# A fused two-block network on one core: the first weight unit loaded and split in halves, the order of VectorE's and ScalarE's work at the start of the expert stage, and one gate multiplication at the end

## The reference, cut to what matters

```python
def swiglu(h, w_in, w_out):
    gate, up = jnp.split(h @ w_in, 2, axis=-1)
    return (jax.nn.silu(gate) * up) @ w_out

def first_block(x, ...):                      # depth 2
    h = h + 0.5 * swiglu(rmsnorm(h, norm_ffn1[i]), ffn1_w_in[i], ffn1_w_out[i])
    ...                                       # conv or dilated attention, then another swiglu

def second_block(x, c, ...):
    mod = jax.nn.silu(c) @ mod_w[l] + mod_b[l]
    ...                                       # h = h + gate_m * hybrid_mixer(...)
    xf = _rms_norm(h, norm_ffn_w[l]) * (1.0 + scale_f) + shift_f
    h = h + gate_f * _hierarchical_moe(xf, ...)
    return _rms_norm(h, norm_out_w)

def _hierarchical_moe(xm, ...):
    # softmax over 4 groups, top 1; softmax over its 4 experts, top 2; comb = their weights
    for gi in range(N_GROUPS_2):
        act = jax.nn.silu(hg) * hu * comb[:, gi, :, None]
        out = out + jnp.einsum('tef,efd->td', act, w_down[gi])
```

## Time and profile before

| | us |
|---|---|
| median of three runs | 1887.58 |
| the profiled execution's own time | 1887.4 |
| its span | 1885.2 |
| TensorE busy | 1849.6 (98%) |
| VectorE busy | 1220.2 (65%) |
| ScalarE busy | 943.4 (50%) |
| mean granted TensorE clock | 0.988 of full |

### The profile page before, as it was taken

How to read it: one execution, slowest core, us unless ns; L and a number is a source line. 1 busy time by engine, 2 the same in 40 slices (tenths; PEclk the granted TensorE clock), 3 DMA queues, 4 the chain that set the end, 5 groups by cost and what they waited for, 6 DMA issues and landing times.

```text
span 1885.2 us, 24482 instructions
## 1 busy us (share of the span) xinstructions
PE 1849.6 (98%) x9398; PEld 1529.7 (81%) x9398; DVE 1220.2 (65%) x1308; ACT 943.4 (50%) x1037; POOL 117.4 (6%) x142
## 2 busy tenths in 40 slices
PE   8999999999999999999999999999999999999997
PEld 6888998888888888888888888898988788876764
DVE  4566666566644557665556566787655766868677
ACT  5443435344544355544445434564445455667574
POOL 0100000000000000000100000223100050000000
PEclk9999899999999999999999999999999999999998
DMA  6877455777555547555644777544233357879695
GB/s 232 292 250 244 144 187 170 235 260 249 169 170 189 186 159 215 179 179 179 90 73 160 246 244 260 170 157 146 101 119 136 111 209 249 324 247 343 248 337 188
DMA packets 239272, 379.16 MB, mean 201 GB/s; under 512 B 13511, under 2 KB 149069, under 8 KB 239184
## 3 DMA queue, kind: packets, MB, share of 16 engines
q1 hardware_dynamic: 233728, 365.13, 57.0%
q0 software_dynamic: 5456, 12.81, 4.0%
HBM read 372.83 MB, written 10.30 MB: 203 GB/s over the span
## 4 chain that ended last, share of the span: by engine, by line
PE 93%; DVE 4%; ACT 1%; DMA 1%; issue 0%; SPq 0%; POOLq 0%; ACTq 0%; DVEq 0%
PE ps L374 27%; PE ps L376 27%; PE ps L375 27%; PE ps L1057 2%; PE ps L1079 1%; PE ps L2790 1%; PE ps L761 1%; PE ps L1067 1%; DVE lo L357 1%; PE ps L1548 1%; PE ps L1035 1%; ACT hi L351 0%; PE ps L1563 0%; PE ps L2837 0%; PE ps L488 0%; PE ps L811 0%
## 5 line engine op out<-in xcount | busy, mean ns | idle before, releaser
L357 DVE TENSOR_TENSOR lo<-raw,hi 128x2048 fp32r<-128x2048 f32 x296 | 679.1, 2299 | 323.2 <-ACT hi L351 322.2
L351 ACT ACTIVATE hi<-raw 128x2048 fp32r<-128x2048 f32 x296 | 565.3, 1915 | 370.0 <-PE ps L376 361.7
L374 PE MATMUL ps<-hi,xT_hi 128*128 128x512 f32 x1376 | 549.9, 400 | 8.1 <-DVE lo L357 5.6
L376 PE MATMUL ps<-hi,xT_lo 128*128 128x512 f32 x1376 | 538.2, 391 | 0.0
L375 PE MATMUL ps<-lo,xT_hi 128*128 128x512 f32 x1376 | 538.2, 391 | 0.0
L374 PEld LDWEIGHTS ps<-hi,xT_hi 128*128 128x128 f32 x1376 | 259.8, 189 | 62.1 <-DVE lo L357 6.1
L376 PEld LDWEIGHTS ps<-hi,xT_lo 128*128 128x128 f32 x1376 | 259.4, 188 | 56.0
L375 PEld LDWEIGHTS ps<-lo,xT_hi 128*128 128x128 f32 x1376 | 259.9, 189 | 49.4
L374 PE MATMUL ps<-hi,ffn_hhi 128*128 128x512 f32 x352 | 137.8, 391 | 0.0
L375 PE MATMUL ps<-lo,ffn_hhi 128*128 128x512 f32 x352 | 137.1, 389 | 0.0
L376 PE MATMUL ps<-hi,ffn_hlo 128*128 128x512 f32 x352 | 137.0, 389 | 0.0
(11 more groups left out here) (453 smaller groups left out, 2248.1 us busy)
## 6 DMA issues: line engine op xcount, KB each, us to landing
raw<-in_ffn_w_in SPq DMA_DIRECT2D x176, 512.0 KB, 4.5
raw<-in_ffn_w_out SPq DMA_DIRECT2D x88, 512.0 KB, 4.1
raw<-in_attn_w_qkv SPq DMA_DIRECT2D x72, 512.0 KB, 4.5
raw<-in_w_in SPq DMA_DIRECT2D x64, 512.0 KB, 4.3
modraw<-in_mod_w SPq DMA_DIRECT2D x48, 512.0 KB, 6.7
raw<-in_w_gate SPq DMA_DIRECT2D x48, 512.0 KB, 4.3
raw<-in_w_up SPq DMA_DIRECT2D x48, 512.0 KB, 5.4
raw<-in_w_down SPq DMA_DIRECT2D x48, 512.0 KB, 4.5
```

The lines of the kernel that those rows point to most:

```text
L351: nc.scalar.activation(hi[u % SPLIT][:, :], raw[raw_slot(u)][:, :], ACT.Copy).then_inc(S("hi_ready"), 1)
L357: nc.vector.tensor_tensor(lo[u % SPLIT][:, :], raw[raw_slot(u)][:, :], hi[u % SPLIT][:, :].bitcast(F32), ALU.subtract).then_inc(S("lo_read ...
L374: nc.tensor.matmul(dst, w_hi, x_hi, start=start, stop=False, skip_group_check=True)
L376: return nc.tensor.matmul(dst, w_lo, x_hi, start=False, stop=stop, skip_group_check=True)
```

## The change

Four things are altered.

1. *First unit in halves.* Unit 0 is loaded by four DMAs of 256 KB in place of two of 512 KB: k = 0, 1 of both column groups first (semaphore `first_half_loaded`), then k = 2, 3. ScalarE rounds it in two instructions of 128x1024 after parts 0 and 1 of `x` rather than one of 128x2048 after all four; VectorE splits it likewise, between parts 1 and 2. TensorE starts with k = 0, 1 of tile 0 once the first half is split, and waits for the whole unit before k = 2.
2. *Expert stage, position 1.* VectorE copies `gathered(1, 1)` and splits block 0's inner activations (`inner_lo(0)`) ahead of the rank tables, and copies `gathered(1, 3)` between the two token tiles' tables. ScalarE does `inner_hi(0)` ahead of rounding unit (1,3) rather than behind it.
3. *Expert stage, position 2.* The groups of `info` come one unit sooner on TensorE (after units (2,0), (2,1), (2,2) rather than (2,1), (2,2), (2,3)). VectorE does `inner_lo(3)`, then `block_info("info_rest", ...)`, then splits D0; before, it split D0, then did `block_info`, then `inner_lo(3)`.
4. *The end.* `y_back`'s copies are added for both tiles first; then the sums in PSUM are added to them, and one multiplication by the gate row and one addition to `h` per tile do for both. `add_gated` is no longer called here.

Some semaphores are also merged into others (`gd_ld` into `gd_small`, `cs_ready` and `conv_pad` into counters shared with the new ones); what waits for what is the same there.

```diff
         def round_unit(act, u, it=None, per=0):
-            if it is None and ("a", u) in done:
+            if it is None and (u == 0 or ("a", u) in done):
                 return
...
+        def first_unit_act(act):
+
+            act.wait_ge(S("first_half_loaded"), 32)
+            nc.scalar.activation(hi[0][:, 0:UNIT // 2], raw[0][:, 0:UNIT // 2], ACT.Copy).then_inc(S("first_half_hi"), 1)
+            act.wait_ge(S("raw_loaded0"), 32)
+            nc.scalar.activation(hi[0][:, UNIT // 2:UNIT], raw[0][:, UNIT // 2:UNIT], ACT.Copy).then_inc(S("hi_ready"), 1)
+
+        def first_unit_dve(dve):
+
+            dve.wait_ge(S("first_half_hi"), 1)
+            nc.vector.tensor_tensor(lo[0][:, 0:UNIT // 2], raw[0][:, 0:UNIT // 2], hi[0][:, 0:UNIT // 2].bitcast(F32),
+                                    ALU.subtract).then_inc(S("first_half_lo"), 1)
+            dve.wait_ge(S("hi_ready"), 1)
+            nc.vector.tensor_tensor(lo[0][:, UNIT // 2:UNIT], raw[0][:, UNIT // 2:UNIT], hi[0][:, UNIT // 2:UNIT].bitcast(F32),
                                     ALU.subtract).then_inc(S("lo_ready"), 1)
...
         def tok_unit(pe, u, half, banks, fresh=None, it=None, per=0, between=None):
 
-            pe_wait_unit(pe, u, it, per)
+            if u:
+                pe_wait_unit(pe, u, it, per)
+            else:
+                pe.wait_ge(S("first_half_lo"), 1)
...
+                if u == 0 and (t, k) == (0, 2):
+                    pe_wait_unit(pe, u, it, per)
...
+                if n == 0 and i == 1:
+                    first_unit_act(act)
...
+                if u == 0:
+                    for k in range(2):
+                        for g in range(2):
+                            sp.dma_start(dst[:, 2 * k:2 * k + 2, g, :], in_src(i, it, half, g)[:, 2 * k:2 * k + 2, :]).then_inc(
+                                S("raw_loaded0" if k else "first_half_loaded"), 16)
+                    return
...
-                    round_unit(act, u)
                     if n == 1 and i == 3:
                         inner_hi(0)
+                    round_unit(act, u)
...
                     split_unit(dve, u)
                     if n == 1 and i == 2:
+                        gathered(1, 1)
+                        inner_lo(0)
                         for t in range(TT):
                             then(permuted(t, 1, place2))
                             then(permuted(t, 2, weight2))
+                            if t == 0:
+                                gathered(1, 3)
...
-                    if n == 1 and i == 3:
-                        inner_lo(0)
...
+                        if n == 2 and i == 0:
+                            inner_lo(3)
+                            block_info("info_rest", slice(2, N_ROUTED), "weight_rest", "dest_rest")
                         split_unit(dve, u)
-                        if n == 2 and i == 0:
-                            block_info("info_rest", slice(2, N_ROUTED), "weight_rest", "dest_rest")
-                            inner_lo(3)
...
+            for t in range(TT):
+                wait_acc(dve, DNU[0][1], t)
+                for c in range(2):
+                    y = y_back[:, t, 0, c * 512:c * 512 + 512]
+                    nc.vector.tensor_tensor(y, y, ps[:, 2 * t + c, :], ALU.add).then_inc(S("gated"), 1)
+                dve.wait_ge(S("gated"), 4 + 2 * t + 2)
                 then(nc.vector.tensor_tensor(y_back[:, t, 0, :], y_back[:, t, 0, :], gate_row[:, 1, :], ALU.mult))
-                then(nc.vector.tensor_tensor(h[:, t, :], h[:, t, :], y_back[:, t, 0, :], ALU.add))
+                nc.vector.tensor_tensor(h[:, t, :], h[:, t, :], y_back[:, t, 0, :], ALU.add).then_inc(S("h_ready"), 2)
...
-                    if n == 2 and i:
-                        info(*((2, 3, 4, 5), (6, 7, 8, 9, 10), range(11, N_POS))[i - 1])
+                    if n == 2 and i < 3:
+                        info(*((2, 3, 4, 5), (6, 7, 8, 9, 10), range(11, N_POS))[i])
...
-            add_gated(dve, DNU[0][1], 1, ysb_all, 1, (0, 1, 2, 3))
```

More of the change, by code:

```diff
@@ L104, in build @@
                            ("gd_s", 1), ("gd_out0", 1), ("ret_out0", 1), ("gd_ws", 1), ("gd_out1", 1), ("ret_out1", 1)),
+            "first_scalar": (("first_half_hi", 1), ("cs_ready", 1)),
+            "first_vector": (("first_half_lo", 1), ("conv_pad", 1)),
             "moe_vector": (("rt_gx", 1), ("rt_sx", 1), ("chosen", 2), ("order_ready", 1), ("rank_read", 1), ("slot_ready", 2), ("xtok_lo", 4),
@@ L353, in split_unit @@
         def split_unit(dve, u, it=None, per=0):
-            if it is None and ("s", u) in done:
+            if it is None and (u == 0 or ("s", u) in done):
                 return
@@ L357, in split_unit @@
             nc.vector.tensor_tensor(lo[u % SPLIT][:, :], raw[raw_slot(u)][:, :], hi[u % SPLIT][:, :].bitcast(F32),
+                                    ALU.subtract).then_inc(S("lo_ready"), 1)
+        def first_unit_act(act):
[9 more added lines that the diff above has]
+            nc.vector.tensor_tensor(lo[0][:, UNIT // 2:UNIT], raw[0][:, UNIT // 2:UNIT], hi[0][:, UNIT // 2:UNIT].bitcast(F32),
                                     ALU.subtract).then_inc(S("lo_ready"), 1)
@@ L929, in conv_dve @@
             nc.vector.memset(vpad[:, :, 0:2], 0.0).then_inc(S("conv_pad"), 1)
-            dve.wait_ge(S("conv_pad"), 1)
+            dve.wait_ge(S("conv_pad"), AT["conv_pad"] + 1)
             def mix(i):
@@ L2011, in gdn_dve @@
                 nc.vector.tensor_tensor(th(GX)[:, t, :], ps[:, 6, T + t * 8:T + t * 8 + 4], row(DTB, 4), ALU.add).then_inc(S("gd_x"), 1)
+        DECAY_STEPS = 22
         def gdn_decay_pool(pool):
@@ L2034, in gdn_decay_pool @@
             then(nc.gpsimd.tensor_tensor(row(SP_), row(LNP), row(RELU), ALU.add))
+            assert steps[0] == DECAY_STEPS
             for t in range(TT):
-                nc.gpsimd.tensor_tensor(th(LD)[:, t, :], th(SP_)[:, t, :], row(NEA, 4), ALU.mult).then_inc(S("gd_ld"), 1)
+                nc.gpsimd.tensor_tensor(th(LD)[:, t, :], th(SP_)[:, t, :], row(NEA, 4), ALU.mult).then_inc(S("gd_small"), 1)
         def gdn_rec_dve(dve):
@@ L2049, in gdn_decay_dve @@
         def gdn_decay_dve(dve):
-            dve.wait_ge(S("gd_ld"), 2)
+            dve.wait_ge(S("gd_small"), DECAY_STEPS + TT)
             nc.vector.tensor_copy(ldB[:, :, :, :].rearrange("p t h n -> p (t h) n"), spread(row(LD), P)).then_inc(S("gd_ldb"), 1)
@@ L2609, in moe_dve @@
                                             xtok_hi[:, t, c * 512:c * 512 + 512].bitcast(F32), ALU.subtract).then_inc(S("xtok_lo"), 1)
+            copied = set()
             def gathered(m, f):
-                if f % 2:
+                if f % 2 and (m, f) not in copied:
+                    copied.add((m, f))
                     dve.wait_ge(S("fill_lo_mm"), fill_no(m, f))
@@ L2991, in _ @@
             act.wait_ge(S("cols_ready"), 2)
-            tiles_act(act, 0, cols[:, COL["ffn1"]:COL["ffn1"] + KT], U0["ffn0"], (0, 1, 2))
+            tiles_act(act, 0, cols[:, COL["ffn1"]:COL["ffn1"] + KT], U0["ffn0"], (1, 2))
             nc.scalar.activation(cs[:, :], cols[:, COL["c"]:COL["c"] + KT], ACT.Silu).then_inc(S("cs_ready"), 1)
@@ L3035, in _ @@
                 tile_dve(dve, 0, half, t, cols[:, COL["ffn1"]:COL["ffn1"] + KT])
-            split_ahead(dve, U0["ffn0"], (0, 1, 2))
+                if (half, t) == (0, 1):
+                    first_unit_dve(dve)
+            split_ahead(dve, U0["ffn0"], (1, 2))
             rstd_dve(dve, 0)
-            dve.wait_ge(S("cs_ready"), 1)
+            dve.wait_ge(S("cs_ready"), AT["cs_ready"] + 1)
             ffn_dve(dve, F0, mod_raw, mod_part, mod_acc, 0, beside_second=bias_dve)
```

## The result

The changed kernel took 1869.97 us in the median of six runs (1866.51 to 1898.42; the last is one disturbed run, which the ratio leaves out, and the median of the other five is 1867.75), and the kernel before, in six runs, 1880.09 us (1877.70 to 1887.96). The ratio is 0.993, 95% interval 0.9904 to 0.9956: 0.7% faster, about 13 us, and by the interval 8 to 18. Forecast were 1871.7 us and a gain of 15.9. The time lies in the forecast range, but the gain is smaller than forecast: the profiled execution that the sum was made against, 1887.4 us, is among the longest runs of its own kernel.

A forecast was written before the change was run, and what follows sets the result against it. TensorE, busy 98% of the span, was taken as the bound, with its waits, half-clock stretches and VectorE's end chain to cut. Gains 5.9 + 4.3 + 3.2 + 2.5 = 15.9 us off 1887.6 gave 1871.7 us, range 1863 to 1879.

The forecast's parts named there:

- I take the clock as full: Start: TensorE idles only from 11.1 to 12.2, so unit 1 starts at 18.45, gaining 5.9 us; 5.1 if the clock falls.
- Does it reach the end?: Behind the start: whether the 5.9 us survive; claimed nothing later becomes late, the nearest by 0.8 us.
- the 1.7: Expert stage, position 1: 3.4 us at half clock behind the 2.6 us wait, costing 1.7 us, goes with that wait.
- What was next late: Position 1: inner_lo(0) waits for ScalarE's inner_hi(0), done at 1525.7, so VectorE idles 0.75 us.
- 12.6 and 10.3: The end: summed VectorE times in us before and after the change; the gain was stated as two 128x1024 instructions, 2.5 us.
- the profiled execution took 1887.4, 0.2 below the median: Base of the sum: the profiled run taken as typical, so 15.9 us was subtracted from a median of 1887.6 us.
- The clock elsewhere, spared: Rival, behind the start: other half-clock stretches vanish, up to 8.7 us more gained, 1863.0 us; chance 0.13.
- D0 too late: Rival, position 2: D0's split over 0.4 us late, TensorE waits some 0.5, clock falls; gain there 1.0, 1873.9 us; chance 0.10.
- the start given back: Rival: unit 1 or step 0's product late; 3 of 5.9 us left and position 1 gains only its wait, 1876.3 us; chance 0.08.
- the weights as the bound: Rival, 1810 to 1850: weight loads don't move with TensorE, position 1 and 2 gains are waited out; 1879.2 us; chance 0.06.
- The 2 us that smaller DMAs might have cost: Start: if the 256 KB quarters added their fixed DMA time in full, the start would gain 3.9 us, the whole 13.9.
- The clock worse at more bridges: Rival, bridges between stages: four more each fall to half clock for 10.2 us, adding 20.5 us, 1892 us; chance 0.05.

The follow-up runs named there:

- tables_only: The kernel before with only the expert-stage position 1 change (copies and inner split of block 0 ahead of and between the rank tables): 1875.86 us, ratio 0.9970.
- sums_only: The kernel before with only the position 2 change (slot sums one unit sooner, D0's split after inner split and sums): 1878.66 us, ratio 0.9990.
- end_only: The kernel before with only the change at the end (one multiplication by the gate): 1879.40 us, ratio 0.9979.
- late_split: The changed kernel with one useless 128x1024 addition on VectorE right ahead of D0's split: 1867.43 us, ratio 0.9927 to the kernel before.
- split_cols: The changed kernel with the 32 one-column matmuls between ffn1's end and ffn2 in two groups of 16: 1867.07 us, ratio 0.9926 to the kernel before.
- after_again: The changed kernel run once more, unchanged: 1868.06 us, ratio 0.9941 to the kernel before.
- copy_only: The kernel before with only the copy gathered(1, 1) moved ahead of the rank tables: 1880.79 us, ratio 0.9994.
- warm_bridge: The changed kernel with unread matmuls among x's transposes and between ffn0 and conv, and one-column matmuls in two groups: 1864.12 us, ratio 0.9908 to the kernel before.

## Why the prediction was right

**The start, 5.9 forecast, 4.35 in the profiled pair.** Every step up to the first product held: ScalarE's halves 1.11 and 1.06 us (1.0 and 1.0 forecast), the second half ready without a wait (0.2 to 0.3 us for it in six other traces), first product at 12.11 (12.2). The step that was mis-sized is "I take the clock as full". I looked at the idle time from 11.1 to 12.2 alone and allowed a fall at 14.7. In after it fell at 10.3, among the transposes, ahead of the first product. Unit 0 then took 7.9 us, not 5.5. The prediction put unit 1 "near 19.3" for the case that the clock falls all the same; its own terms, 12 products 0.43 us apart and 12 at 0.227, give 12.2 + 7.9 = 20.1, and 20.01 was measured. The cause that it gave for the old fall, TensorE without work from 11 to 16.4, is doubtful as well: in tables_only, sums_only and end_only, which have the same old start, the clock fell at 10.3, 11.2 and 9.7 us, ahead of that wait. The 18.45 forecast for unit 1 was reached within 0.45 in late_split and split_cols, the same code with a full clock. So the start is worth 4.35 or about 5.9 by what the clock does; after_again, with 3.4 us of half clock, gains 5.3. "Does it reach the end?" held to 0.0 us: 1489.4 in both.

**Part 2, 4.3 forecast, 4.47.** The wait and the 1.7 us behind it both went. What was next late was named rightly: VectorE idles 0.86 us for `inner_hi(0)` (0.75 forecast), and no fill waits. copy_only shows why it takes three moves. What I put down as certain and is not is the 1.7: in sums_only and end_only the same wait cost its own 2.5 and 2.6 us and no clock. Part 2 is worth 2.7 or 4.5 us by execution.

**Part 3, 3.2 forecast, 3.19.** Of these 1.6 are the wait, and 1.6 the clock, which fell in before and copy_only but not in tables_only and end_only. The split of D0 was the right thing to fear: its margin is 0.2 to 0.33 us.

**Part 4, 2.5 forecast, 2.47.** Two instructions of 128x1024 less on VectorE, which in both traces works without a wait of over 0.2 us from the landing of `y_back` to its last instruction. (The prediction's 12.6 and 10.3 differ by 2.3 only; its count of two instructions is what came true.)

**The median.** The parts sum to 14.5 in the profiled pair. The medians, 1880.09 and 1867.75, differ by 12.3, and the ratio makes it about 13. The step that failed here is "the profiled execution took 1887.4, 0.2 below the median": with three runs the median was one of two at 1888, while most later runs lie at 1878 to 1883. The execution profiled had the falls behind both expert waits and 20.5 us more at half clock, 27.3 us in all, which cost 13.7, and I counted 3.4 us of that cost as what the change takes away. In an execution without these falls it takes away none of it. With the start at 5.3 on average (24.2 over the six traces with the old start, 18.9 over the four with the new), the waits alone at 2.7 and 1.6, and 2.5 at the end, the change is then worth 12.1 us, and 15.5 where both stretches go with the waits. The timed runs bear this out, if they are paired by my own grouping: the two longest before (1887.58 and 1887.96) and the two longest after (1872.18 and 1872.91) are 15.2 us apart, the other four and three, 1877.70 to 1880.89 and 1866.51 to 1867.75, 11.9. On another chip the runs of the kernel before spread from 1877.5 to 1888.6 without such a gap.

That 1871.7 came close to the measured time owes something to luck. Against the middle of the runs the base was 7.5 us too high and the gain some 3 too large, and the two errors offset each other in part; the range around it was wide enough for what was left, 4 us to the median of the five.

**The rivals.** The clock elsewhere, spared: it is in after_again, by 5.1 us. D0 too late, the start given back, the weights as the bound: none was seen, and 291.57 us from position 3 to TensorE's last matmul in all traces speaks against the third. The 2 us that smaller DMAs might have cost, which the prediction worked out and left out of its sum, aren't seen either: the first half of unit 0 had landed by 9.4 us in after, the first DMA of 512 KB in before by 9.8. The clock worse at more bridges: in no trace. One thing that no rival names moves the end by as much as a part of the change: `y_back`'s first addition starts up to 2.1 us sooner or later against TensorE's last matmul, by when it lands.

## What to carry to other kernels

Where a queue in fixed order has a long block without a waiter close behind it, here 4 us of tables, put the short copies that another engine waits for ahead of it and in its middle; moving only the first moves the wait to the second. Cut a trace into pieces at points that every version has, and compare piece by piece: a gain of 0.1% that timings can't resolve is plain there to 0.1 us, as far as the clock is the same in both. Before summing against one profiled execution, see where it lies among the runs, and count what a wait costs in clock only as often as traces show it.

## What the runs showed of the hardware

- The same instructions at the same place run at full or at half clock by execution: unit 0 took 7.9 us in after (12.11 to 20.01) and 6.2 in split_cols (11.83 to 18.01), of which its 24 products, 0.227 us apart, take 5.5 and the wait for unit 1 the rest. Two executions of one kernel had 20.5 and 10.2 us at half clock between the same two points.
- A TensorE that is busy throughout can fall to the 1.2 GHz level: 30.00 of 30 us busy, clock 0.89, with 32 matmuls of one column ahead of the fall, which took 4.78 us. In six of eleven executions the same block had no fall.
- Half clock comes by execution: the falls near 505 and near 1201 and those behind the expert waits of 2.6 and 1.5 us came together or not at all, over fourteen traces.
- Matmuls whose result nobody reads, with the one-column block in two groups, keep the clock up: granted clock 0.996 to 0.998 in six runs of warm_bridge, 0.990 to 0.995 in six of after_again.
- The clock fell at 10.3 us in after, among the transposes ahead of the first product, though TensorE had been idle for at most 1.1 us at a time. In split_cols, with the same transposes and idle times of up to 1.1 us, it didn't.
- Two DMAs of 256 KB in place of one of 512 KB cost nothing visible: in late_split unit 0's quarters had landed by 8.6, 9.8, 9.9 and 11.15 us, in before its two DMAs by 9.8 and 11.1. In after ScalarE's first half started at 9.69, right behind its transposes, with no wait for it.
